# Token sums of the first column tiles on VectorE, two weight halves in places of their own, the silu table loaded at the start

## The reference

```
def swiglu(h, w_gate, w_up, w_down):
    return (jax.nn.silu(h @ w_gate) * (h @ w_up)) @ w_down

h = swiglu(rmsnorm(x, ffn1_pre_g[l]), ffn1_w_gate[l], ffn1_w_up[l], ffn1_w_down[l])
x = x + 0.5 * rmsnorm(h, ffn1_post_g[l])
...                       # the mixer: x = x + rmsnorm(y, mix_post_g[l])
h = swiglu(rmsnorm(x, ffn2_pre_g[l]), ffn2_w_gate[l], ffn2_w_up[l], ffn2_w_down[l])
x = x + 0.5 * rmsnorm(h, ffn2_post_g[l])
```

## Time and profile before

| | us |
|---|---|
| median of 3 runs | 1795.06 |
| lowest and highest run | 1794.76, 1795.96 |
| the profiled execution | 1796.16 |
| its span, first to last instruction | 1794.4 |
| TensorE busy | 1771.8 (99%) |
| VectorE busy | 1452.8 (81%) |
| ScalarE busy | 952.4 (53%) |
| GpSimd busy | 171.1 (10%) |

### The profile page before, as it was taken

One profiled execution on the slowest core, in us unless ns is written; L12 is line 12 of the kernel. 1 busy time (PEld: TensorE's weight loads), 2 busy tenths in 40 slices (PEclk: granted clock), 3 DMA queues, 4 the chain that ended last, 5 costly groups with the idle time before them and its releaser, 6 DMA issues.

```text
span 1794.4 us, 20287 instructions
## 1 busy us (share of the span) xinstructions
PE 1771.8 (99%) x8106; PEld 1470.4 (82%) x8106; DVE 1452.8 (81%) x1433; ACT 952.4 (53%) x1011; POOL 171.1 (10%) x193
## 2 busy tenths in 40 slices
PE   8999999999999999999999999999999999999998
PEld 7788888888888888888888887888888888888886
DVE  6999999999888777755755548999999999887776
ACT  4755555555555445743234446555655555565543
POOL 3011111111000000350000002011111111000000
PEclk9999999999999999999999999999999999999999
DMA  7566666666566665665454654666666666565664
GB/s 258 179 208 196 203 200 199 200 206 204 178 209 199 199 199 198 214 185 156 131 150 126 208 171 164 204 207 199 200 199 202 208 198 202 192 195 188 210 201 151
DMA packets 155774, 345.37 MB, mean 192 GB/s; under 512 B 10568, under 2 KB 11152, under 8 KB 155296
## 3 DMA queue, kind: packets, MB, share of 16 engines
q1 hardware_dynamic: 154832, 339.79, 60.4%
q0 software_dynamic: 736, 4.26, 0.7%
q10 hardware_dynamic: 112, 0.03, 0.0%
HBM read 341.94 MB, written 2.10 MB: 192 GB/s over the span
## 4 chain that ended last, share of the span: by engine, by line
PE 94%; DVE 2%; ACT 1%; DMA 1%; issue 1%; DVEq 0%; POOLq 0%; POOL 0%; SPq 0%; ACTq 0%
PE ps L1371 21%; PE ps L1373 21%; PE ps L1372 21%; PE ps L1569 7%; PE ps L1571 7%; PE ps L1570 7%; PE ps L1642 2%; PE ps L1639 2%; PE ps L1641 2%; PE ps L1742 1%; PE ps L1521 1%; DVE wlo L854 1%; DMA raw<-in_ffn_w_down_dram 1%; DVE x L1105 1%; ACT xT_hi L528 0%
## 5 line engine op out<-in xcount | busy, mean ns | idle before, releaser
L854 DVE TENSOR_TENSOR wlo<-raw,whi 128x1024 fp32r<-128x1024 f32 x440 | 545.6, 1262 | 165.0 <-ACT whi L468 162.5
L468 ACT ACTIVATE whi<-raw 128x1024 fp32r<-128x1024 f32 x440 | 457.6, 1056 | 311.4 <-DMA raw<-in_ffn_w_down_dram 155.7
L1371 PE MATMUL ps<-whi,xT_hi 128*128 128x512 f32 x1088 | 431.2, 396 | 8.5 <-DVE wlo L854 5.9
L1373 PE MATMUL ps<-whi,xT_lo 128*128 128x512 f32 x1088 | 425.4, 391 | 0.0
L1372 PE MATMUL ps<-wlo,xT_hi 128*128 128x512 f32 x1088 | 424.8, 390 | 0.0
L1371 PE MATMUL ps<-whi,hT_hi 128*128 128x512 f32 x672 | 262.4, 391 | 2.8 <-DVE wlo L854 2.8
L1373 PE MATMUL ps<-whi,hT_lo 128*128 128x512 f32 x672 | 261.5, 389 | 0.0
L1372 PE MATMUL ps<-wlo,hT_hi 128*128 128x512 f32 x672 | 261.5, 389 | 0.0
L1371 PEld LDWEIGHTS ps<-whi,xT_hi 128*128 128x128 f32 x1088 | 205.2, 189 | 53.5 <-issue 8.6
L1373 PEld LDWEIGHTS ps<-whi,xT_lo 128*128 128x128 f32 x1088 | 205.0, 188 | 43.6
L1372 PEld LDWEIGHTS ps<-wlo,xT_hi 128*128 128x128 f32 x1088 | 205.2, 189 | 40.8
(11 more groups left out here) (188 smaller groups left out, 2531.7 us busy)
## 6 DMA issues: line engine op xcount, KB each, us to landing
raw<-in_ffn_w_down_dram SPq DMA_DIRECT2D x136, 512.0 KB, 3.7
raw<-in_ffn_w_gate_dram SPq DMA_DIRECT2D x96, 512.0 KB, 3.8
raw<-in_ffn_w_up_dram SPq DMA_DIRECT2D x96, 512.0 KB, 3.7
raw<-in_w_in_dram SPq DMA_DIRECT2D x80, 512.0 KB, 3.7
srawB<-in_ffn_w_gate_dram SPq DMA_DIRECT2D x40, 512.0 KB, 4.8
srawB<-in_ffn_w_up_dram SPq DMA_DIRECT2D x40, 512.0 KB, 4.8
srawA<-in_ffn_w_gate_dram SPq DMA_DIRECT2D x40, 512.0 KB, 4.6
srawA<-in_ffn_w_up_dram SPq DMA_DIRECT2D x40, 512.0 KB, 4.6
```

The costliest lines, as they stand in the source:

```text
L468: nc.scalar.activation(whi[:, slot(g), :], raw[:, slot(g), :], ACT.Copy).then_inc(hi_ready, 1)
L854: V.tensor_tensor(wlo[:, slot(g), :], raw[:, slot(g), :], whi[:, slot(g), :].bitcast(f32), ALU.subtract).then_inc(lo_ready, 1)
L1371: mm(bank, a_hi, whi[:, s, c0:c0 + NT], start=start, stop=False, skip_group_check=skip)
L1373: return mm(bank, a_lo, whi[:, s, c0:c0 + NT], start=False, stop=stop, skip_group_check=skip)
```

## The change

It has four parts, in both up stages alike where not said otherwise.

1. `token_sums` moves from GpSimd to VectorE, in three pieces: the addition over 128x2048, two of the sums, and the other two. In FFN1 they stand behind the `wlo` of halves 7, 8 and 9. In FFN2 the first piece stands before the `wlo` of half 8, and the others behind halves 9 and 10. Their split on ScalarE moves to half 11 (FFN1) and 12 (FFN2), on VectorE to 11 and 13.
2. In the second column tile the first two gate halves are used one after the other, before the first group. Both (numbers 16 and 17) get places of their own outside the ring (`raw2`, `wlo2`, `whi2`), are loaded right behind half 15, and are converted before the group's sums. In FFN1 the blocks of the first group are loaded behind half 9 instead of 11.
3. The dummy activation at the very start of ScalarE's program is a silu instead of a copy.
4. In all twenty later tiles VectorE makes the low part of half 4 before that of the third group's sums. In the first tile the block sums and their low parts come apart (`block_t`, `block_lo`).

```
+HSEQ = {1: (0, 2, 1, 3, 4, 5, 6, 7)}
+def half_of(j, h):
+    return divmod(HSEQ[j][h] if j in HSEQ else h, 2)
...
 def slot(g):
     for b, d in ((U1, D1), (U2, D2)):
         if b + 16 <= g < d:
-            return (g - b) % 4
+            return RING + g - b - 16 if g < b + 18 else (g - b) % 4
...
     @block.sync
-                    if h == 11:
+                    if h == (11 if f else 9):
                         sums(1, 0)
+                half(1, 0)
+                half(1, 1)
                 sums(1, 1)
-                for h in range(4):
-                    half(1, h)
+                half(1, 2)
+                half(1, 3)
...
     @block.scalar
         def first_tile(b):
-                    if h == (9 if f else 14):
+                    if h == (12 if f else 11):
                         act.wait_ge(sf_ok, f + 1)
                         nc.scalar.activation(S_hi[:]..., Sf[:, 0:3]..., ACT.Copy).then_inc(sfhi_ok, 1)
-                    if h == 14:
+                    if h == (12 if f else 11):
                         act.wait_ge(w_used, b + 2 * NS)
                         nc.scalar.activation(xT_hi[:, 0:2 * NS:2, P:2 * P], Sf[:, 3], ACT.Copy).then_inc(sfhi_ok, 1)
-                    if h == 15:
-                        if not f:
-                            x_square(3)
-                        sum_hi(f, 1, 0)
+                    if not f and h == 14:
+                        x_square(3)
                 half_hi(b, 1, 0)
                 half_hi(b, 1, 1)
+                sum_hi(f, 1, 0)
...
-            nc.scalar.activation(nat[:, 0, 0:1], ident[:, 0:1], ACT.Copy)
+            nc.scalar.activation(nat[:, 0, 0:1], ident[:, 0:1], ACT.Silu)
...
     @block.vector
+            def token_sums(f, part):
+                a11, a12, a21, a22 = (xf[:, :, c, t * P:(t + 1) * P] for t in range(TOK) for c in range(2))
+                if part == 0:
+                    if f:
+                        dve.wait_ge(u_lo, 24)
+                    else:
+                        dve.wait_ge(x_lo, NS)
+                    V.tensor_tensor(xf[:]..., xT_hi[:, 0:2 * NS, :].bitcast(f32),
+                                    xT_lo[:, 0:2 * NS, :].bitcast(f32), ALU.add).then_inc(xf_ok, 1)
+                if part == 1:
+                    dve.wait_ge(xf_ok, f + 1)
+                    V.tensor_tensor(Sf[:, 2], a21, a11, ALU.subtract)
+                    link(V.tensor_tensor(Sf[:, 0], a21, a22, ALU.add))
+                if part == 2:
+                    link(V.tensor_tensor(Sf[:, 1], Sf[:, 0], a11, ALU.subtract))
+                    V.tensor_tensor(Sf[:, 3], a12, Sf[:, 1], ALU.subtract).then_inc(sf_ok, 1)
...
         def up_tile(b, j):
                 block_sums(f, j, 2)
+                half_lo(b, j, 4)
                 sum_lo(f, j, 2)
-                half_lo(b, j, 4)
...
     @block.tensor
                 for j in range(1, FTILES):
                     half(b, j, 0)
-                    products(f, j, 0)
-                    half(b, j, 1)
+                    if j == 1:
+                        half(b, j, 1)
+                        products(f, j, 0)
+                    else:
+                        products(f, j, 0)
+                        half(b, j, 1)
```

More of the change, by code:

```diff
@@ L127, in build @@
     whi = at("whi", 32, [P, RING, 1024], f32r)
+    raw2 = at("raw2", 72, [P, 2, 1024])
+    wlo2 = at("wlo2", 72, [P, 2, 1024], f32r)
+    whi2 = at("whi2", 80, [P, 2, 1024], f32r)
     hT = at("hT", 64, [P, FC, SEQ])
@@ L237, in build, with raw_of, hi_of, lo_of @@
         out_kc = list(range(KC // 2, KC)) + list(range(KC // 2))
+        def raw_of(g):
+            return raw[:, slot(g), :] if slot(g) < RING else raw2[:, slot(g) - RING, :]
+        def hi_of(g):
+            return whi[:, slot(g), :] if slot(g) < RING else whi2[:, slot(g) - RING, :]
+        def lo_of(g):
+            return wlo[:, slot(g), :] if slot(g) < RING else wlo2[:, slot(g) - RING, :]
         def flat(ap):
@@ L261, in half @@
                 def half(j, h):
-                    load(b + 16 + 2 * PLAIN * (j - 1) + h, part(h % 2, NS + h // 2, j))
+                    i, m = half_of(j, h)
+                    load(b + 16 + 2 * PLAIN * (j - 1) + h, part(m, NS + i, j))
                 def sums(j, s):
@@ L381, in load_gain @@
                 pool.dma_start(gpost[:], gain[0:1, :].broadcast_to([P, D])).then_inc(gain_in, 16)
[L383 to L395, removed]
             def group_sums(f):
@@ L592, in first_tile @@
                         block_hi(f, 1, 0)
-                    if h == (9 if f else 14):
+                    if f and h in (9, 11):
+                        unit_hi(2, G_FFN2, h // 2 + 2)
+                        unit_square(4, 2, h // 2 + 2)
+                    if h == (12 if f else 11):
                         act.wait_ge(sf_ok, f + 1)
@@ L1031, in first_tile @@
                         V.tensor_copy(vcol[:, VEARLY:VROWS], ps[JUNK][:, 0:VROWS - VEARLY]).then_inc(vcol_ok, 1)
-                    if h == (10 if f else 14):
+                    if not f and h in (7, 8, 9):
+                        token_sums(f, h - 7)
+                    if h == (13 if f else 11):
                         token_sums_lo(f)
-                    if h == 13:
-                        block_sums(f, 1, 0)
-                    if h == 14:
+                    if f and h == 13:
+                        mean_square(k, x_sq, 24)
+                    if h == 15:
                         last_token_sum_lo(f)
@@ L1039, in first_tile @@
                         unit_lo(2, G_FFN2, h // 2 + 2)
-                mean_square(k, x_sq, 24 if f else 8)
-                sum_lo(f, 1, 0)
+                    if f and h in (9, 10):
+                        token_sums(f, h - 8)
+                    if h == (12 if f else 13):
+                        block_t(f, 1, 0)
+                    if h == 14:
+                        block_lo(f, 1, 0)
+                    if not f and h == 14:
+                        mean_square(k, x_sq, 8)
                 half_lo(b, 1, 0)
                 half_lo(b, 1, 1)
+                sum_lo(f, 1, 0)
             def up_tile(b, j):
@@ L1183, in to_ffn2 @@
                 unit_lo(2, g0, 5)
+                token_sums(1, 0)
                 lo(b + 8)
@@ L1367, in _, with three @@
             mm = nc.tensor.matmul
-            def three(bank, a_hi, a_lo, s, c0, start, stop, skip=False):
-                mm(bank, a_hi, whi[:, s, c0:c0 + NT], start=start, stop=False, skip_group_check=skip)
-                mm(bank, a_hi, wlo[:, s, c0:c0 + NT], start=False, stop=False, skip_group_check=skip)
-                return mm(bank, a_lo, whi[:, s, c0:c0 + NT], start=False, stop=stop, skip_group_check=skip)
+            def three(bank, a_hi, a_lo, g, c0, start, stop, skip=False):
+                w_hi, w_lo = hi_of(g)[:, c0:c0 + NT], lo_of(g)[:, c0:c0 + NT]
+                mm(bank, a_hi, w_hi, start=start, stop=False, skip_group_check=skip)
+                mm(bank, a_hi, w_lo, start=False, stop=False, skip_group_check=skip)
+                return mm(bank, a_lo, w_hi, start=False, stop=stop, skip_group_check=skip)
             def narrow_half(g, n, banks):
@@ L1601, in half @@
                         ins = three(ps[2 * m + t][:], xT_hi[:, k, t * P:(t + 1) * P], xT_lo[:, k, t * P:(t + 1) * P],
-                                    slot(g), c * NT, i == 0 and c == 0 and not (m == 1 and t == 0),
+                                    g, c * NT, i == 0 and c == 0 and not (m == 1 and t == 0),
                                     c == 1 and (i == PLAIN - 1 or i == PLAIN - 2 and m == 1 and t == 1), True)
```

37 lines of the change are left out of this document (20 added, 17 removed).

## The result

The changed kernel takes 1784.68 us (median of 4 runs, 1784.58 to 1785.09) beside 1795.51 us for the kernel before on the same chip (4 runs, 1794.76 to 1796.83). The ratio is 0.9939, 95% interval 0.9922 to 0.9957: faster by 0.6%, 10.8 us between the medians, where 10.9 were forecast. The profiled execution took 1784.65 us.

A forecast was written before the change was run, and what follows sets the result against it. TensorE bounds the kernel, busy 1771.8 of 1794.4 us; 4.35 + 1.64 + 5.46 - 0.5 = 10.9 us off the 1795.06 median gives 1784.2 us, range 1782.7 to 1788.8.

The forecast's parts named there:

- Place A: FFN1, half 4: TensorE waits for `wlo` while GpSimd's addition holds up VectorE; 2.75 plus 1.60 us low clock, 4.35 back.
- Place B: FFN1, after half 15: TensorE waits for the first gate bank's silu, late on ScalarE; 1.64 us given back.
- ScalarE's chain: FFN1, before the first silu: ScalarE's last conversion ends at 60.1, silu 0.66, handing over 0.15, TensorE served at 60.95.
- Place C: FFN2, halves 6 to 8: GpSimd's addition delays VectorE's residuals; waits and 1.68 us low clock, 5.46 us given back.
- The chain of 22.0 us: FFN2, VectorE's work from 1101.4 through half 15's `wlo`, ending at 1124.4 with 1 us waiting; TensorE there at 1124.3.
- The 0.5 us kept back: Deduction from the gain: 0.4 us for waits in FFN2's halves 13 to 15, 0.1 us at the first silu in FFN1.
- The `pow` behind VectorE: GpSimd's small `pow` making `rr` for the silu: if held up by three VectorE instructions, silu up to 1 us late.
- Group 1 after two halves: Second tile: group 1 comes 2.72 us later, delaying group 3's loads; taken as 0, up to 1 us per FFN.
- The order of `wlo` 4: All twenty tiles: group 3's low sums end 1.16 us later, within 4.4 us of reserve; no effect on time.
- The check of the tile behind: Sign to look for in the tile after the first: no wait for `sloA` or `sloB`.
- The low clock: Low-clock stretches behind waits at half 4 of FFN1 and half 8 of FFN2: 1.60 and 1.68 us, booked as recovered.

The follow-up runs named there:

- e5: The changed kernel with one 128x2048 addition, its result unused, put back on GpSimd at its old place in each FFN: 1794.08 us, 0.9994 of the kernel before.
- e6: The changed kernel with a GpSimd memset of 128x2048, which reads nothing, where GpSimd's addition stood in each FFN: 1785.30 us, 0.9947 of the kernel before.
- e1: The kernel before with only the dummy activation made a silu: 1792.99 us, 0.9995 of the kernel before.
- e3: The kernel before with the token sums on VectorE and the dummy activation a silu, nothing else: 1789.82 us, 0.9977 of the kernel before.
- e4: The changed kernel with the dummy activation a copy again: 1786.09 us, 0.9959 of the kernel before.
- e7: The changed kernel without the own places for halves 16 and 17, which use the ring again, all orders kept: 1789.23 us, 0.9973 of the kernel before.
- e8: e3 with the first block's sums and their low parts split around a half on VectorE: 1787.80 us, 0.9963 of the kernel before.
- e11: The changed kernel with group 3's low sums ahead of half 4's low part again in all twenty tiles: 1786.00 us, 0.9956 of the kernel before.
- e9: The changed kernel unaltered, timed again on another chip: 1785.46 us, 0.9950 of the kernel before.
- e2: The kernel before with only the token sums moved to VectorE: 1790.79 us, 0.9981 of the kernel before.

## Why the prediction was right

**Place A** was right in mechanism and size. e5 shows the cause alone: one addition on GpSimd brings all of it back. e6 adds that an operation which only writes doesn't do it.

**Place B** came out at 1.64 as forecast, and ScalarE's chain was right: the silu was to start at 60.1, or 55.6 with the 4.46 gained by then, and it started at 55.61. But the two parts that I named there have no shares of their own. The early table alone gives back 0.89 (e1's step is 0.98 where it was 1.87). What is left, 0.75, is a wait for the `wlo` of half 16, and e3 has it too: VectorE makes a 2.29 us low part ahead of that `wlo`. It goes with the halves ahead of the block, in whose order VectorE makes that `wlo` first. And the table, taken out of the finished change, costs 1.42 (e4: a step of 1.65). The parts mend one chain and their shares don't add.

**Place C** was right as a sum and wrong as an account. I booked 5.46 to the token sums, as an upper bound, on the ground that "nothing else in those stretches waits". That holds for halves 6 to 8 (5.58, 0.1 over the bound), and not for what comes behind them: with the token sums and the table alone (e3) TensorE loses 4.46 of it again at half 14. The chain of 22.0 us that I added up for VectorE had the right total (the `wlo` of half 15 was to end at 1124.4, or 1118.7 with the 5.69 gained by then; it ended at 1119.1), and a total doesn't see where a `wlo` stands in it. What keeps C is the splitting of the block's sums (e7 has it without the own places, e8 without the two halves ahead, and neither has the wait of e3 at half 14), which I had not priced at all. Since the kernel as a whole had it, the forecast came out.

**The 0.5 us kept back.** A step of 0.39 at half 14 of FFN2, 0.16 lost; nothing at B.

**The `pow` behind VectorE.** I held it harmless, and at most 1 us late. It is harmless in the changed kernel (0.71 us in FFN1, 1.61 in FFN2), where the mean square is made earlier. e8, where it isn't, shows what I feared: 2.6 us, and the silu late. That the earlier mean square alone makes this difference is argued from the two traces, not run.

**Group 1 after two halves.** I took 0 and "up to 1 us per FFN". It cost 0.3 in one FFN. The sign of the mechanism was right; the reserve on TensorE took most of VectorE's 1.82.

**The order of `wlo` 4.** Nothing in the steady tiles, as said; 0.8 us in the two second tiles if it is left as it was (e11).

**The check of the tile behind**, no wait for `sloA` or `sloB`, is met by the list of waits, though the two slow steps of 0.42 and 0.34 us lie there.

**The low clock** is the term that the comparison left least certain. I priced it at 3.28 in the two places, as the profiled execution shows it. In e1's profile TensorE stands as long at A, and its clock doesn't fall, nor does it at C:

```profile
21.94 0.39 PE L1373 MATMUL ps<-whi,xT_lo 128*128 128x512 f32 x1
24.93 0.47 PE L1371 MATMUL ps<-whi,xT_hi 128*128 128x512 f32 x1 [2.60 <-DVE wlo L854]
25.24 0.39 PE L1372 MATMUL ps<-wlo,xT_hi 128*128 128x512 f32 x1
25.47 0.39 PE L1373 MATMUL ps<-whi,xT_lo 128*128 128x512 f32 x1
```

Fifty-four timed runs of the kernel before, beside e1 to e11, say the same. Those with a mean clock of 0.999 have a median of 1792.81 us (12 runs), those with 0.998 one of 1794.33 (28 runs), those with 0.997 one of 1795.98 (13 runs), and one run with 0.996 took 1797.08. So of the 10.9 us, some 7 to 8 are there in every run (1792.81 less the changed kernel's 1784.68 is 8.1, less the 1785.46 of e9 is 7.4; the prediction's sum without its low clock is 7.6), and some 3 come and go. The kernel before ran at 1795.51 in the first comparison and at 1794.07 beside e9, which fits more low stretches in the first; of the kernel before only the clock of the profiled execution is on record there (0.997, at 1796.16 us). The other 0.8 us between 0.9939 and 0.995 is the changed kernel itself, slower in e9, and has no cause that the runs show. It stays within 1.7 us in its nine runs, with no such wait left. The sentence that the stretches "come and go with the waits" was too strong: without a wait there was none, but not every wait had one. The Trainium skill, TensorE: Matmul & The Clock Gate, "What's actually happening", which I cited against my own term, says that the gate's monitor runs free of the program; by that rule it is chance whether one and the same wait brings the clock down, and the traces agree.

## What to carry to other kernels

When a long stall of one engine goes, the next engine's queue is met earlier by as much, so add it up instruction by instruction up to each tile that is waited for, not as one total; parts of a change that mend one chain have no shares of their own. An engine that is shut out shows as a few instructions of several times their usual length that end with the other engine's operation; an operation on that other engine which only wrote did no harm here. A wait can also move a small operation onto the chain, as the `pow` in e8: look at the row of the engine that isn't named. A low clock behind a wait of 2 to 3 us is a loss with a chance, to be counted at less than its size in one trace.

## What the runs showed of the hardware

- A 128x2048 addition on GpSimd with both inputs in SBUF takes 5.5 to 5.6 us and stretches a VectorE subtraction beside it from 1.2 to 5.6 us, a residual from 0.70 to 5.1. A memset of 128x2048 by GpSimd takes 1.82 us and stretches nothing.
- A `pow` on GpSimd over 128x2 took 0.71 us where VectorE stood idle, 1.61 beside the end of one VectorE subtraction and the start of the next (FFN2, changed kernel), and 2.6 to 2.7 beside a low part of 2.28 us (e8).
- The clock after waits at the level of one trace: it fell behind waits of 2.75 (A before and in e5), 2.88 (e2), 3.10 us (e3) and 2.4 to 2.5 us (C, before and e5), and did not behind waits of 2.76 and 2.37 (A and C in e1), 2.08 and 1.80 us (e7). The last two are not cleared by one trace: three of e7's eight runs have a lower mean clock (0.998, 0.998, 0.997) and take 1790.38, 1791.05 and 1793.57 us.
- The table switch costs 1.41 us of ScalarE's time: from the start of the conversion ahead of the silu to the start of the silu it is 3.22 us in e4 and 1.81 in the changed kernel. 1.28 of it are the load's row, the silu starts 0.02 us after the row, and the rest is that the silu otherwise starts 0.10 us before the row ahead of it ends.
